# Attention of a two-layer hybrid trunk: from one head and chunk at a time to units of two heads side by side

## What is computed

```
C (MoBA): q, k of 64; scores q.k * 64^-0.5
          past blocks of 256 keys by top-3 gate, and the causal own block;
          with 512 tokens there are two blocks, so each query sees its whole past
D (MLA):  q, k = 64 + 32 rotary columns; scores * 96^-0.5, causal
both:     p = softmax(scores);  out = p @ v   (v of 64)
y = concat(A, B, C, D) @ W_out
```

## Time and profile before

| | before |
|---|---|
| median of 3 runs | 1233.34 us |
| the profiled execution | 1234.61 us, its span 1232.8 us |
| instructions | 15490 |
| PE, DVE, ACT, POOL busy | 97%, 66%, 47%, 17% of the span |
| chain that ended last | PE 79%, DVE 10%, POOL 4% of the span |
| idle of PE before products (L523) for a DVE low part of `xn` | 8.6 us |

### The profile page before, as it was taken

How to read it: one execution, slowest core, us unless ns; L and a number is a source line. 1 busy time by engine, 2 the same in 40 slices (tenths; PEclk the granted TensorE clock), 3 DMA queues, 4 the chain that set the end, 5 groups by cost and what they waited for, 6 DMA issues and landing times.

```text
span 1232.8 us, 15490 instructions
## 1 busy us (share of the span) xinstructions
PE 1196.1 (97%) x6004; PEld 1005.9 (82%) x6004; DVE 815.6 (66%) x1160; ACT 581.5 (47%) x883; POOL 204.6 (17%) x190
## 2 busy tenths in 40 slices
PE   6999998999999999999999999999999999999997
PEld 6887877888888888888888877878888888888886
DVE  4699767578666666544758887657766666664454
ACT  4455466545444444434545645756444444443442
POOL 1275155110000000000005732612000000000000
PEclk9999999999999999999999999999999999999999
DMA  8233322534333333466633324135333333326573
GB/s 246 73 85 85 90 44 99 166 112 120 101 88 103 92 96 103 155 195 214 193 97 90 87 82 101 68 108 160 94 103 103 97 92 103 92 96 200 175 224 134
DMA packets 155035, 146.84 MB, mean 119 GB/s; under 512 B 4783, under 2 KB 135763, under 8 KB 154963
## 3 DMA queue, kind: packets, MB, share of 16 engines
q1 hardware_dynamic: 154384, 145.12, 39.0%
q10 hardware_dynamic: 579, 0.74, 0.2%
HBM read 139.54 MB, written 2.10 MB: 115 GB/s over the span
## 4 chain that ended last, share of the span: by engine, by line
PE 79%; DVE 10%; POOL 4%; issue 3%; ACT 2%; DMA 1%; POOLq 0%; DVEq 0%; ACTq 0%
PE ps L523 26%; PE ps L525 25%; PE ps L524 25%; DVE wsp L425 2%; POOL rms_r L878 1%; POOL cf_out L887 1%; DVE ps L1157 1%; PE ps L774 1%; PE ps L799 1%; DVE yt L958 1%; PE ps L585 1%; POOL prob L904 1%; ACT wsp L417 1%; DVE rot L1034 1%; POOL wsp L425 1%
## 5 line engine op out<-in xcount | busy, mean ns | idle before, releaser
L523 PE MATMUL ps<-xn,wsp 128*128 128x512 f32 (+1 forms) x1120 | 412.7, 368 | 8.6 <-DVE xn L978 8.6
L425 DVE TENSOR_TENSOR wsp<-raw,wsp 128x1024 fp32r<-128x1024 f32 (+2 forms) x250 | 307.2, 1231 | 160.3 <-ACT wsp L417 160.1
L524 PE MATMUL ps<-xn,wsp 128*128 128x512 f32 (+1 forms) x1120 | 409.9, 366 | 0.0
L525 PE MATMUL ps<-xn,wsp 128*128 128x512 f32 (+1 forms) x1120 | 409.8, 366 | 0.0
L417 ACT ACTIVATE wsp<-raw 128x1024 fp32r<-128x1024 f32 (+2 forms) x256 | 266.1, 1041 | 167.7 <-PE ps L525 128.6
L523 PEld LDWEIGHTS ps<-xn,wsp 128*128 128x128 f32 x1120 | 212.6, 190 | 43.8 <-DVE xn L978 9.9
L525 PEld LDWEIGHTS ps<-xn,wsp 128*128 128x128 f32 x1120 | 212.5, 190 | 34.0
L524 PEld LDWEIGHTS ps<-xn,wsp 128*128 128x128 f32 x1120 | 212.6, 190 | 33.9 <-issue 0.5
L523 PE MATMUL ps<-wsp,hid 128*128 128x512 f32 (+1 forms) x488 | 189.9, 389 | 0.4 <-DVE wsp L425 0.4
L525 PE MATMUL ps<-wsp,hid 128*128 128x512 f32 (+1 forms) x488 | 189.1, 387 | 0.0
L524 PE MATMUL ps<-wsp,hid 128*128 128x512 f32 (+1 forms) x488 | 189.0, 387 | 0.0
(11 more groups left out here) (150 smaller groups left out, 1302.8 us busy)
## 6 DMA issues: line engine op xcount, KB each, us to landing
raw<-in_w_ffn_up SPq DMA_DIRECT2D x88, 512.0 KB, 3.8
raw<-in_w_ffn_down SPq DMA_DIRECT2D x88, 512.0 KB, 4.2
raw<-in_w_in SPq DMA_DIRECT2D x36, 512.0 KB, 3.9
raw<-in_w_out SPq DMA_DIRECT2D x32, 512.0 KB, 3.4
x<-in_x SPq DMA_DIRECT2D x4, 512.0 KB, 8.3
xn<-xn SPq DMA_DIRECT2D x8, 256.0 KB, 3.3
out_x<-x SPq DMA_DIRECT2D x4, 512.0 KB, 4.1
raw<-in_w_vkr SPq DMA_DIRECT2D x4, 432.0 KB, 3.7
```

What stands on the lines that cost most here:

```text
L425: eng.tensor_tensor(wsp[:, u % SPLIT, 1, 0:nk * n], raw[:, (l * NU + u) % RAW, 0:nk * n], fp(wsp[:, u % SPLIT, 0, 0:nk * n]), ALU.subtract ...
L523: pe.matmul(dst, a[0], b[0], start=start, stop=False, skip_group_check=True)
L524: pe.matmul(dst, a[0], b[1], start=False, stop=False, skip_group_check=True)
L525: return pe.matmul(dst, a[1], b[0], start=False, stop=stop, skip_group_check=True)
```

## The change

Heads are taken in pairs (0 and 1, 2 and 3, ...). A unit is one head of a pair in one of three parts: chunks 0 and 1 together, chunk 2, chunk 3. There are 24 units a layer, and at every even step PE makes the scores of two units, the two heads of a pair in the same part, into two of four banks. For MoBA the matmuls of the two heads alternate (rows 0 to 63 and 64 to 127 of the array); for MLA they follow one another.

The causal mask is no longer added by DVE. PE starts each accumulation with a matmul of the identity by a 128 x 128 mask over the diagonal block (`mask`). The scales 64^-0.5 and 96^-0.5 are put into the keys when these are split. DVE takes the negated maximum straight from PSUM, and ACT makes the exponential straight from PSUM; `sm` is gone, and `prob` has five buffers instead of three.

Unread products are left only in the first three steps, two in each, into the second transpose bank. The values of a pair are made in three parts (both heads' chunks 0 and 1; the second head's chunks 2 and 3; the first head's), 6, 10 and 11 steps after the first step of the pair, in front of that step's transposes; the first head's product is 64 columns wide and overwrites rows 0 to 63 of what the second's wrote. ACT and DVE take both heads in one copy. POOL splits the first three W_out units in halves. The first two rows of W_out are multiplied at steps 25 and 26, before the last transposes and values. ACT makes two copies (identity and mask) once at the start.

The diff, cut to its core, without the indentation that all lines of a part share; where a part shows only lines that are added, those they take the place of stand in the kernel above.

```diff
@@ -143,11 +143,36 @@
 CF_VECTOR = {3: 2, 4: 1, 5: 1, 6: 1, 7: 1, 8: 4, 9: 4, 10: 4, 11: 2, 12: 4, 13: 4, 14: 3}
 CF_SCALAR = {3: 1, **{g: 3 for g in range(4, 14)}}
 assert sum(CF_VECTOR.values()) == CF_TAPS and sum(CF_SCALAR.values()) == CF_TAPS
-N_ATT = 2 * HEADS * TC
-NPROB = 3
+PARTS = ((0, 1), (2,), (3,))
+PAIRS = HEADS
+STEPS = 2 * len(PARTS)
+N_UNIT = PAIRS * STEPS
+N_ROW = 2 * HEADS * TC
+NPROB = 5
 TRAIL = 3
-VALUES_AFTER = (3, 5, 6)
+VALUES_AT = (3, 7, 8)
+PV_TAKEN = 9
 ATT_TAIL = TRAIL + 5
+OUT_HI, OUT_LO = (8, 11, 14), (9, 10, 12, 13, 15, 16)
+OUT_EARLY = {N_UNIT + 1: 0, N_UNIT + 2: 1}
+def unit(t):
+    pair, r = divmod(t, STEPS)
+    return pair, r // 2, r % 2
+def chunks_of(t):
+    pair, part, i = unit(t)
+    return [(slice((c == 1) * P, ((c == 1) + c + 1) * P), (2 * pair + i) * TC + c) for c in PARTS[part]]
+def blocks_of(t):
+    return sum(c + 1 for c in PARTS[unit(t)[1]])
 def hybrid_trunk_kernel(nc, inp, rope_tables, out):
...
+        pt_early = hid[:, PT:PT + 2, :, :].rearrange("p a b t -> p (a b t)")[:, 0:12 * P]\
+            .rearrange("p (n s t) -> p n s t", n=2, s=2)
         pt_late = hid[:, PT + 2:PT + 6, :, :].rearrange("p a b t -> p (a b t)")\
             .rearrange("p (n s k t) -> p n s k t", n=2, s=2, k=4)
-        def pt_of(h, c, s):
-            tile = pt_early if c < 2 else pt_late
-            return tile[:, h % 2, s, 0:c + 1, (c % 2) * P:(c % 2 + 1) * P]
+        def pt_of(t, s):
+            _, part, i = unit(t)
+            if part == 0:
+                return pt_early[:, i, s, :].rearrange("p (k t) -> p k t", t=P)
+            return pt_late[:, i, s, 0:part + 2, (part - 1) * P:part * P]
...
+PRODUCTS = ((0, 0), (0, 1), (1, 0))
+def mask(t):
+    bank, part = SCORE_BANKS[t % 4], unit(t)[1]
+    if part == 0:
+        pe.matmul(ps[:, bank, :].rearrange("p (c k) -> p c k", c=2)[:, :, 0:P], ident_r[:, :],
+                  causal_r[:, :].unsqueeze(1).broadcast_to([P, 2, P]), start=True, stop=False,
+                  skip_group_check=True)
+    else:
+        pe.matmul(ps[:, bank, (part + 1) * P:(part + 2) * P], ident_r[:, :], causal_r[:, :],
+                  start=True, stop=False, skip_group_check=True)
 def scores(t):
...
+    pair, part, _ = unit(t)
+    if t == 0:
+        bank_free(l, G_MK)
+        bank_free(l, G_MV)
+    elif t == 2:
+        bank_free(l, G_MV + 1)
     else:
...
+        pe.wait_ge(exp_done, l * N_UNIT + t - 2)
+    if t == N_UNIT // 2:
+        pe.wait_ge(keys_moved, (l + 1) * 32)
+        pe.wait_ge(queries_moved, (l + 1) * 32)
+        pe.wait_ge(kr_placed, (l + 1) * 64)
+        pe.wait_ge(rope_placed, (l + 1) * 64)
+    chunks = list(zip(PARTS[part], chunks_of(t)))
+    if pair < PAIRS // 2:
+        q, k = hid[:, QM + pair], hid[:, KM + pair]
+        for i in range(2):
+            mask(t + i)
+        for c, (cols, _) in chunks:
+            for a, b in PRODUCTS:
+                for i in range(2):
+                    r = slice(DH * i, DH * i + DH)
+                    last = pe.matmul(ps[:, SCORE_BANKS[(t + i) % 4], cols], q[r, a, c * P:(c + 1) * P],
+                                     k[r, b, 0:(c + 1) * P], start=False, stop=a == 1, skip_group_check=True)
+                    if a and c == PARTS[part][-1]:
+                        last.then_inc(score_done, 1)
     else:
...
         r = slice(0, MLA_QK)
...
+        for i in range(2):
+            h = 2 * (pair - PAIRS // 2) + i
+            q, k = ml_q[h], ml_k[h]
+            mask(t + i)
+            for c, (cols, _) in chunks:
+                last = product(ps[:, SCORE_BANKS[(t + i) % 4], cols],
+                               (q[r, 0, c * P:(c + 1) * P], q[r, 1, c * P:(c + 1) * P]),
+                               (k[r, 0, 0:(c + 1) * P], k[r, 1, 0:(c + 1) * P]), False, True)
+            last.then_inc(score_done, 1)
+def keep_clock(bank):
+    pe.matmul(ps[:, bank, :], ident_r[:, :], vm[:, 0, 0:2, :].rearrange("p c d -> p (c d)"),
+              start=True, stop=True, skip_group_check=True)
 def transposes(t):
...
+    bank = PT_BANKS[t % 2]
     if t >= 2:
...
+        pe.wait_ge(pt_ready, l * N_UNIT + t - 1)
+    elif t == 0:
+        bank_free(l, G_MQ + 1)
+    pe.wait_ge(prob_done, l * N_UNIT + t + 1)
+    for b in range(blocks_of(t)):
+        last = pe.transpose(ps[:, bank, b * P:(b + 1) * P], prob[:, t % NPROB, b * P:(b + 1) * P],
+                            ident[:, :])
     last.then_inc(pt_done, 1)
...
+def values(pair, part):
+    g = G_PV + pair
     if part < 2:
...
+        pe.wait_ge(pt_ready, l * N_UNIT + STEPS * pair + (2, STEPS)[part])
     if part == 0:
...
+        bank_free(l, g - 2 if pair >= 2 else (G_MR, G_MQ)[pair])
+    v = vm if pair < PAIRS // 2 else vl
+    c0 = pair % 2 * P
+    for i in ((1, 0), (1,), (0,))[part]:
+        m = P if i else DH
+        for kc in range(4 if part else 2):
+            skip = P if kc == (3 if part else 1) else 0
+            out_cols = slice((part > 0) * 2 * P + skip, ((part > 0) * 2 + 2) * P)
+            probs = [pt_late[:, i, s, kc, skip:2 * P] if part else pt_early[:, i, s, 2 * kc * P:(2 + kc) * P]
+                     for s in range(2)]
+            last = product(ps[0:m, bank_of(g), out_cols], [v[:, s, kc, c0:c0 + m] for s in range(2)], probs,
+                           kc == 0, skip > 0)
+    if part == 0:
+        last.then_inc(pv_early, 1)
     if part == 2:
         last.then_inc(group_done, 1)
...
+def out_row(half, k):
+    if half == 0 and k == 0:
+        pe.wait_ge(y_ready, l * 4 + 4)
+        pe.wait_ge(exp_done, (l + 1) * N_UNIT)
+    if half == 0 and k >= KD - 2:
+        bank_free(l, G_PV + k - 4)
+    if half == 1 and k == 0:
+        pe.wait_ge(pt_ready, (l + 1) * N_UNIT)
+    row_product(l, U_OUT + half * KD + k, k, KD, MIX, half)
 pe.wait_ge(qk_ready, l * 4 + 4)
...
+if l == 0:
+    pe.wait_ge(mask_set, 2)
+for t in range(N_UNIT + ATT_TAIL):
+    if t < N_UNIT and t % 2 == 0:
         scores(t)
...
+    if t < TRAIL:
+        if t == 0:
+            bank_free(l, G_MK + 1)
+        for _ in range(2):
+            keep_clock(PT_BANKS[1])
+    for hp in range(PAIRS):
+        if t - TRAIL - STEPS * hp in VALUES_AT:
+            values(hp, VALUES_AT.index(t - TRAIL - STEPS * hp))
+    if TRAIL <= t < N_UNIT + TRAIL:
         transposes(t - TRAIL)
...
+    if t in OUT_EARLY:
+        out_row(0, OUT_EARLY[t])
 for half in range(2):
     for k in range(KD):
...
+        if half == 0 and k < len(OUT_EARLY):
+            continue
         if half == 0 or k < KD - LAST_ROWS:
...
+            out_row(half, k)
         elif k == KD - LAST_ROWS:
             last_rows(l, U_OUT + KD, KD, MIX)
...
@@ -898,19 +975,34 @@
 pool.wait_ge(rot_sin, l + 1)
 pool.tensor_tensor(ml_rot[:, :], ml_rot[:, :], ml_shuf[:, :], ALU.add).then_inc(rot_done, 1)
...
+def out_lo_part(i, part):
+    u = U_OUT + i
+    cols = slice(part * HALF, (part + 1) * HALF)
+    pool.wait_ge(hi_done, l * NU + u + 1)
+    ins = pool.tensor_tensor(wsp[:, u % SPLIT, 1, cols], raw[:, (l * NU + u) % RAW, cols],
+                             fp(wsp[:, u % SPLIT, 0, cols]), ALU.subtract)
+    if part == 0:
+        ins.then_inc(lo_half, 1)
+    else:
+        ins.then_inc(lo_done, 1)
+for t in range(N_UNIT):
+    pool.wait_ge(inv_done, l * N_UNIT + t + 1)
+    for cols, row in chunks_of(t):
+        last = pool.tensor_tensor(prob[:, t % NPROB, cols], prob[:, t % NPROB, cols],
+                                  rowinv[:, row:row + 1].to_broadcast([P, cols.stop - cols.start]), ALU.mult)
+    last.then_inc(prob_done, 1)
+    if t == 1:
         pool.wait_ge(rot_hi, l * 5 + 5)
         pool.tensor_tensor(ml_rope[:, 1, :], ml_rot[:, :], fp(ml_rope[:, 0, :]), ALU.subtract)\
             .then_inc(rope_ready, 1)
...
+    if t in OUT_LO:
+        i, part = divmod(OUT_LO.index(t), 2)
+        if part:
+            pool.wait_ge(lo_half, l * LEAD + i + 1)
+            pool.wait_ge(lo_done, l * NU + U_OUT + i)
+        out_lo_part(i, part)
 for stage in (MIX, FFN):
     for what, c in RMS_ORDER:
         if what == "y" or (l, stage) != (DEPTH - 1, FFN):
...
+                         ALU.mult, ALU.subtract).then_inc(qk_ready, 1)
                 def group_a_lo(c):
...
@@ -1184,40 +1277,28 @@
     dve.tensor_tensor(ml_q[2 * i][:, 1, :], ps[:, bank_of(G_MQ + i), :], fp(ml_q[2 * i][:, 0, :]),
                       ALU.subtract).then_inc(qn_ready, 1)
...
+for t in range(N_UNIT + ATT_TAIL):
+    if t < N_UNIT:
+        dve.wait_ge(score_done, l * N_UNIT + t + 1)
+        for cols, row in chunks_of(t):
+            last = dve.reduce_max(out=negmax[:, row:row + 1], in_=ps[:, SCORE_BANKS[t % 4], cols],
+                                  axis=mybir.AxisListType.X, negate=True)
+        last.then_inc(masked, 1)
+    if 1 <= t <= N_UNIT:
+        first, end = chunks_of(t - 1)[0][1], chunks_of(t - 1)[-1][1] + 1
+        dve.wait_ge(exp_done, l * N_UNIT + t)
+        dve.reciprocal(rowinv[:, first:end], rowsum[:, first:end]).then_inc(inv_done, 1)
+    if TRAIL <= t < N_UNIT + TRAIL:
```

(46 more changed lines are left out.)

165 lines of the change are left out of this document (22 added, 143 removed).

## The result

The changed kernel takes 1218.32 us, the median of four runs (1217.09 to 1219.56); before it was 1233.3. The ratio is 0.9877, its 95% interval 0.986 to 0.9894. The gain is 15 us where 6 were forecast: the time lies in the range, at the value of rival A, but the forecast gain was less than half of the measured one.

The account below looks back on a forecast made before the run. PE, busy for 97% of the span, was taken as the bound. Per layer, work -5.0 us and waits +2.0 us gave -3.0, so -6.0 for two layers: 1233.3 to 1227.3 us, range 1217 to 1235.

Parts of the forecast that it names:

- rival A: Attention: streams and loads of both heads overlap, 64-wide values cost nothing, half the pair stalls go; 1218 to 1221, chance 0.21.
- unread products: PE in attention: 19 unread products a layer become 6, 4.3 to 1.4 us, -2.9.
- MoBA: trips, side by side, its masks: MoBA scores: ten fewer 64-row trips, neighbouring heads partly overlapping, masks added on PE; -4.8 us a layer together.
- MLA scores with masks: MLA scores: same columns, no change, plus causal masks now added by PE; +1.2 us a layer.
- waits: PE in attention: 6.7 us of waits and unresolved rest a layer instead of 4.7, +2.0.
- I take the middle, +1.5: Values 64 columns wide: entering and leaving costs between 0 and 3.0 us a layer; middle taken, +1.5.
- the trip price of 64-row scores: MoBA scores: one trip into 64-row work and out costs PE 0.38 us.
- I take 5.4: MoBA scores side by side: streams overlap, weight loads follow at 0.11 us; 7.6 becomes 5.4 us a layer, -2.2.
- 3.8 in place of 5.4: MoBA scores side by side: price a layer if weight loads of the two heads overlap too, 3.8 us.
- third condition: More-overlap rival: half of the pair stalls in attention gone, 3.0 us.
- B: MoBA scores: the two heads run one after the other, 1232, or 1235 with dear 64-wide values; chance 0.12.
- D: In-order ACT and DVE queues: each of six pairs loses 2.0 us instead of 1.0, gain gone, 1233; chance 0.13.
- C: MoBA half: without the removed products the clock falls, some 9 us a layer slower, 1245; chance 0.07.

Follow-up runs that it names:

- b2: Kernel before with its single unread products only in steps 3 to 7, 11 a layer instead of 19: 1229.17 us.
- e2: Changed kernel with both MoBA heads of a pair on array rows 0 to 63: 1222.31 us.
- e8: Changed kernel without the 24 mask matmuls a layer, so no causal mask: 1215.77 us.
- e3: Changed kernel with the first head's values 128 columns wide in the array instead of 64: 1220.71 us.
- e4: Changed kernel with each step's transposes ahead of the values of the pair before: 1214.06 us.
- b1: Kernel before with no unread product after step 2, 13 of 19 a layer gone: 1245.95 us.

## Why the prediction was right and wrong

| step, us per layer | forecast | measured | by |
|---|---|---|---|
| unread products | -2.9 | -2.9 | 13 x 0.23 from rows; b2 has 0.26 each |
| MoBA: trips, side by side, its masks | -4.8 | -6.5 | 13.7 before; after, 2 pairs x (0.89 + 0.72 + 0.90, and 1.11 for the masks with the three ways in); e2 |
| MLA scores with masks | +1.2 | +1.4 | 8.1 before, 2 x 4.78 after; e8 |
| transposes and values | +1.5 | -2.1 | 3.13 for an MLA head before, x 8; 5.72 to 5.80 for an MLA pair after, x 4; e3 |
| waits | +2.0 | +1.7 | idle time of PE in the stage (from start to start +2.0) |
| sum | -3.0 | -8.4 | stage: -8.2 |

The sum of the parts agrees with the stage to about 0.3 us. The ten trips fewer and the moved mask work were not tested each by itself in the old structure; they are read from rows.

*Wrong, "I take the middle, +1.5" for the 64-wide values.* This step failed most, by 3.6 us a layer. It was bounded by 0 and by the trip price of 64-row scores, and both bounds had the same flaw: fewer rows of the array and fewer columns were taken for the same thing. No way in or out shows, and a load of 64 columns lets the next 128-column matmul follow at 0.06 us. e3 gives 1.1 us a layer back. The cause of the other 0.7 to 1.0 stays open. One reading is that before, the first matmul of each of 24 value parts a layer, behind a transpose, is followed only after 0.20 us where 0.12 is the normal step, and that now fewer parts begin so. But the transposes in front give most of it back. Timeline of PE in before:

```profile
189.67 0.60 PE L774 MATMUL ps<-ident,prob 128*128 128x128 f32 x4
190.03 0.36 PE L523 MATMUL ps<-hid 128*128 128x256 f32 x1
```

Four blocks take 0.36 us there instead of 0.44. No run tests either.

*Wrong, "I take 5.4, because 0.11 is what every row with short matmuls shows as the floor".* This is most of the 1.7 us a layer that the MoBA line missed. That floor is one of loads on the same rows, so it said nothing of loads on different ones. Loads and streams overlap entirely: groups of two heads cost what groups of one did, way in included, and e2 takes this away with the same count, columns and banks. I had the value for it (3.8 in place of 5.4) and gave it 0.21.
The Trainium skill (TensorE: Matmul & The Clock Gate, The mechanism) had said it, as quoted at rival A; e2 against after agrees with it, and it deserved to be the main case.

*Right: masks, unread products, and every wait.* Place and size of the waits held (masks 2.25 us in e8, 2.4 forecast): six waits were forecast, six came, each named by its releaser, though those of the third and fourth pair ended on DVE and not on POOL. ACT's value copy (176.17) stands in front of its copy of the transposes (176.65), so DVE's half and with it PE's bank come late. e4 removed both kinds by moving 1.2 us of PE's work behind the transposes.

*Rival A* was right in its overlap, not in its third condition: no stall went away, and the 3.0 us that it took for that did not come. The values gained more than it allowed them in its place. So its mechanism is half right, and that the time lies in its 1218 to 1221 is partly luck. *B* and *D* did not come. *C* did not come and was no phantom: the same removal in the old structure costs 12.5 us (b1). My argument against it, that the matmul behind a wait of 1.57 us is 0.28 long, was unsound: b1's fell with waits of under 1 us. A clock that holds behind one wait says nothing of another stretch.

So the parts don't add up one by one: in the old structure removing the first five of the single unread products costs 17 us, and in the new one they are gone without harm. What in it holds the clock stays open.

## What to carry to other kernels

Where heads use half of the array's rows, put two on different halves: the pair costs one, and price it so if only the rows differ. Take unread work out in steps and read the granted clock of each, in every layer: some of it is plain work, and without some of it the clock falls. When a stage gets shorter, look at the next buffer that its last instructions free: here the splits of W_out began to wait for the DMA when attention was 8 us shorter, and with one unit split earlier most of them waited for PE again.
